# Two unused constant tables added and two gaps between on-chip tensors removed, in a two-layer-pair transformer kernel

## The reference

```python
for l in range(2):                                   # first kind ("one")
    mod = silu(c) @ ada_w[l] + ada_b[l]              # 9 x 1024 shifts, scales, gates
    h += 0.5 * g1 * swiglu(modulate(rms_norm(h)), ffn1_w_in[l], ffn1_w_out[l])
    z = modulate(rms_norm(h)) @ w_in[l]              # differential attention, convolution,
    h += g2 * concat(o_a, o_b, o_c, o_d) @ w_out[l]  # spatial gating, forgetting attention
    h += 0.5 * g3 * swiglu(modulate(rms_norm(h)), ffn2_w_in[l], ffn2_w_out[l])
for l in range(2):                                   # second kind ("two")
    z = rmsnorm(h) @ w_in_2[l]                       # 24 heads of q, k, v and 3 x 1024 gates
    h += (gates * branches) @ w_o_2[l]               # dilated, block and stick-breaking attention
    h += relu(rmsnorm(h) @ w_up_2[l]) ** 2 @ w_down_2[l]
```

## Time and profile before

| what | value |
|---|---|
| time, median of 3 runs | 2022.61 us (2020.84, 2022.61 and 2032.96) |
| the profiled execution's own time | 2022.61 us |
| span of its trace | 2020.8 us |
| mean granted TensorE clock | 0.982 of full |
| PE busy | 1944.2 us (96%), 15216 matmuls |
| POOL busy | 1320.6 us (65%) |
| ACT busy | 940.4 us (47%) |
| DVE busy | 835.4 us (41%) |
| bytes read by DMA | 394.62 MB, 196 GB/s over the span |

### The profile page before, as it was taken

The page is one execution under the profiler, slowest core; times in us unless marked ns, Lnnn a source line. Parts: engine busy times, 40 slices in busy tenths (PEclk is TensorE's granted clock), DMA queues, the critical chain, the costliest instruction groups (busy, mean ns, idle before and its releaser), DMA issues.

```text
span 2020.8 us, 36133 instructions
## 1 busy us (share of the span) xinstructions
PE 1944.2 (96%) x15216; PEld 1870.4 (93%) x15216; DVE 835.4 (41%) x1747; ACT 940.4 (47%) x1467; POOL 1320.6 (65%) x612
## 2 busy tenths in 40 slices
PE   7999997999999999889999999999999999999999
PEld 3999996899999999779999999989999999989999
DVE  3774577382147466745112622233311622233322
ACT  2544454344454445444444445525543445525543
POOL 0888760388878887316887964506897964505896
PEclk8999998999999999899999999999999999999999
DMA  9999650695589885217545643336664643335662
GB/s 321 359 345 308 198 185 22 207 365 181 185 302 365 279 264 187 84 63 267 192 161 173 209 157 110 125 118 189 200 204 152 209 148 112 124 121 188 199 201 99
DMA packets 357075, 398.01 MB, mean 197 GB/s; under 512 B 9017, under 2 KB 319025, under 8 KB 356913
## 3 DMA queue, kind: packets, MB, share of 16 engines
q1 hardware_dynamic: 356752, 395.50, 59.0%
q10 hardware_dynamic: 160, 0.20, 0.0%
HBM read 394.62 MB, written 1.05 MB: 196 GB/s over the span
## 4 chain that ended last, share of the span: by engine, by line
PE 85%; DVE 4%; SPq 3%; ACT 3%; POOL 2%; DMA 1%; issue 1%; ACTq 0%; DVEq 0%
PE bank L716 67%; PE bank L800 6%; PE bank L1124 3%; POOL w_lo L682 2%; PE bank L929 1%; PE bank L963 1%; SPq L577 1%; SPq L544 1%; DVE bank L1653 1%; PE bank L747 1%; ACT w_hi L1204 1%; DVE arena L1724 1%; PE bank L751 1%; PE bank L1025 1%; SPq L587 1%
## 5 line engine op out<-in xcount | busy, mean ns | idle before, releaser
L682 POOL TENSOR_TENSOR w_lo<-ring,w_hi 128x1024 fp32r<-128x1024 f32 (+2 forms) x608 | 1320.4, 2197 | 685.3 <-ACT w_hi L1204 684.7
L716 PE MATMUL bank<-hn,w_hi 128*128 128x256 f32 x2752 | 773.5, 281 | 5.9 <-POOL w_lo L682 5.0
L1204 ACT ACTIVATE w_hi<-ring 128x1024 fp32r<-128x1024 f32 (+2 forms) x608 | 578.5, 976 | 409.9 <-PE bank L716 368.2
L716 PE MATMUL bank<-hn_lo,w_hi 128*128 128x256 f32 x2752 | 764.8, 278 | 0.0
L716 PE MATMUL bank<-hn,w_lo 128*128 128x256 f32 x2752 | 764.7, 278 | 0.0
L716 PEld LDWEIGHTS bank<-hn,w_hi 128*128 128x128 f32 x2752 | 519.5, 189 | 10.1 <-POOL w_lo L682 6.0
L716 PEld LDWEIGHTS bank<-hn_lo,w_hi 128*128 128x128 f32 x2752 | 518.5, 188 | 1.2 <-issue 0.5
L716 PEld LDWEIGHTS bank<-hn,w_lo 128*128 128x128 f32 x2752 | 518.0, 188 | 0.0
L716 PE MATMUL bank<-gated,w_hi 128*128 128x256 f32 x1408 | 248.9, 281 | 0.0
L716 PEld LDWEIGHTS bank<-gated,w_hi 128*128 128x128 f32 x1408 | 217.0, 190 | 0.0
L716 PE MATMUL bank<-gated,w_lo 128*128 128x256 f32 x704 | 197.8, 281 | 0.0
(11 more groups left out here) (209 smaller groups left out, 2226.1 us busy)
## 6 DMA issues: line engine op xcount, KB each, us to landing
ring<-in_ffn_w_in SPq DMA_DIRECT2D x88, 1024.0 KB, 7.5
ring<-in_w_in SPq DMA_DIRECT2D x72, 1024.0 KB, 5.1
arena<-in_ada_w SPq DMA_DIRECT2D x35, 2048.0 KB, 10.5
ring<-in_w_up SPq DMA_DIRECT2D x32, 1024.0 KB, 5.4
ring<-in_w_down SPq DMA_DIRECT2D x32, 1024.0 KB, 5.1
ring<-in_ffn_w_out SPq DMA_DIRECT2D x32, 768.0 KB, 5.1
ring<-in_ffn_w_out SPq DMA_DIRECT2D x32, 640.0 KB, 4.1
ring<-in_w_in SPq DMA_DIRECT2D x16, 512.0 KB, 3.6
```

The source lines that it names most:

```text
L682: pool.tensor_tensor(w_lo[:, q, ks], ring[:, r, k0:k0 + n], w_hi[:, q, ks], ALU.subtract) \
L716: last = mm(out, a, b, start=start and i == 0, stop=stop and i == 2)
L1204: f(w_hi[:, q, half * 4:half * 4 + n], ring[:, r, k0:k0 + n], ACT.Copy).then_inc(weights_rounded, 1)
```

## The change

The host's table gains a block "before" of 384 columns ahead of "before_neg", and a block "in64" of 2 columns ahead of "in64_eighth". The two unused tensors `hn_start` and `arena_start` go. No instruction is added, removed or moved on any engine, and no wait.

```diff
@@ constant_tables
     before = np.concatenate([before[:P, :], before[P:, P:]], axis=1)
+    put("before", before)
     put("before_neg", np.where(before > 0, 0.0, -2.0 ** 100))
     put("in32", r[:, None] // 32 == np.arange(4)[None, :])
+    put("in64", r[:, None] // 64 == np.arange(2)[None, :])
     put("in64_eighth", (r[:, None] // 64 == np.arange(2)[None, :]) * 0.125)
@@ build
         h = sb("h", KT, S)
-        hn_start = sb("hn_start", 48)
         hn, hn_lo = sb("hn", KT, S, dtype=F32R), sb("hn_lo", KT, S, dtype=F32R)
@@ build
         ident_r, unseen = sb("ident_r", P, dtype=F32R), sb("unseen", P, dtype=F32R)
-        arena_start = sb("arena_start", 80)
         arena = sb("arena", ARENA)
```

## The result

| | before | after |
|---|---|---|
| median | 2027.07 us (4 runs, 2020.84 to 2032.96) | 2055.74 us (4 runs, 2053.22 to 2056.45) |
| the profiled execution | 2022.61 us, span 2020.8 | 2055.16 us, span 2053.4 |

The kernel became slower: the ratio is 1.014, with a 95% interval of 1.0121 to 1.016. The forecast was 2023.2 us, between 2016 and 2037, with no change that can be measured. Both were wrong, and rival A, equal offsets collide, is what happened.

The account below looks back on a forecast made before the run. PE's three-part products at line 716 were taken to bound the kernel, with DMA at the start. 2022.61 us plus 0 for addresses plus 0.6 for table bytes gave 2023.2 us, range 2016 to 2037 us.

Parts of the forecast that it names:

- rival A: Matmuls with `hn`: weight load and moved operand at equal offsets collide, up to 43 us, giving 2066 us; chance 0.14.
- What bounds the kernel: Whole span: PE busy 96%, 85% of the chain, line 716 alone 67%; slower matmuls there count in full.
- The offset of either operand alone is worth nothing: Line 716: offsets 192 and 704 go at 113.3 to 113.4 ns, offset 0 at 114 ns, so 0 us.
- Do equal offsets matter? I take 0 us.: `hn` against its weights: 0 us, since plain float32 takes 215 ns at equal and 216 ns at unequal offsets.
- The upper bound: Most that equal offsets could cost: 4.5 ns for each of 9600 matmuls with `hn` or `hn_lo`, 43 us.
- The bound for a gain: Slow stretches of line 716 all at the fast pace: 13.4 us in the long pieces, perhaps some 20 us.
- The rule of two read ports: TensorE reads the moved operand and the weight load through independent ports, so equal offsets would cost nothing.
- Two paces, set by the last interruption: Line 716 goes at 113.3 or 117.9 ns, set by what interrupted PE last, not by where operands lie.
- The bytes, 0.6 us.: Start, SP's table loads: 197,632 bytes more at 350 GB/s, 0.6 us in full on the path, 1.2 at most.
- DVE and ACT: Reads and writes of `hn`, `square`, `const` and tables at new addresses: 0 us, any cost hidden anyway.
- Rival B: Stretches of line 716 fall out at the other pace: one turned gives 2020 or 2027 to 2030 us; chance 0.20.
- C: Stretches with `hn` lose the slow pace: up to some 20 us faster, 2003 us; chance 0.05.

Follow-up runs that it names:

- tables-alone kernel: The changed kernel with the gap of 48 float32 ahead of `hn` kept and the new table 8 columns narrower; 2034.41 us, ratio 1.0061 against before.

## Why the prediction was wrong

*What bounds the kernel* held: outside the start, each nanosecond of a matmul in line 716 came out in the time in full, and nothing else did.

*The offset of either operand alone is worth nothing.* This held, and more strictly than I had shown it: the same `hn` address is fast against weights at 0 and slow against weights at 192.

*Do equal offsets matter? I take 0 us.* This is the step that failed: the term for equal offsets, put at nothing. The row it stood on, plain float32 at 215 and 216 ns, is true, and holds at all seven offsets that the runs have, but it doesn't carry over to the three-part form. That the load has some 100 ns more to hide there (215 against 113 ns from start to start) may be why; that is argued and was not tried. For the three-part form the price is 6.7 ns over the fast pace and 2.2 over the slow one. I had named the row as weaker than the case asked for, and then drew a chance of 0.14 from it, when the trace said that each pairing it had shown in this form stood at 192 or 64 within 256 bytes, all the good ones. A trace that holds none but the good offsets says nothing about the others. The sign that the prediction gave for A came out to the letter: long pieces with `hn` over 115 ns a matmul, with `up2` still at 113.

*The upper bound* of 4.5 ns for each of 9600 matmuls, 43 us, was the right count with two wrong sizes that partly cancel. The step is 6.7 ns from the fast pace, not 4.5; but those that came from the slow pace, such as the 912 at 583.49 us, lost only 2.2, and 2112 of `gated` gained 4.5 each, 9.5 us. I had not thought of that gain. A's price at half its bound, 2045 us, and its full price, 2066 us, stand on either side of the 2055.74 measured; that it lies so well between them is luck. The bound for a gain had missed the second `x624`, at 691.72 us, which makes it 16.2 us for the long pieces and not 13.4.

*The rule of two read ports* (the Trainium skill, TensorE: Matmul & The Clock Gate, "Step-by-step: what each phase is for") says that loading the next weights doesn't take bandwidth from the running matmul. The runs disagree for this form: the same two streams of reads take 113.3, 117.8, 118.7 or 120.0 ns a matmul by nothing but their offsets. The measurement decides. For plain float32 the runs agree with the rule, with the same 27.88 us for 128 at seven offsets. Whether there are two ports no run here shows; in the three-part form the two streams aren't free of each other.

*Two paces, set by the last interruption* held in part: an interruption turned the pace, but the same one left the piece of 912 slow in one run and fast in another. And it misled me in one place: I concluded from it that the pace is no matter of where operands lie. It is a matter of both. At offsets of 64 and 192 the interruption chooses among two, at 0 and 96 there is only the slow one of 120.

*The bytes, 0.6 us.* The loads read 893.5 KB as foretold:

```profile
const<-in_constants SPq DMA_DIRECT2D x2, 893.5 KB, 14.1
```

but they cost next to nothing. In the tables-alone kernel the last wait for DMA ended 0.2 to 0.4 us later and a faster piece of 96 made up for it. In the changed kernel PE is slower in that stretch and no longer waits for chunks at all:

```profile
126.00:163.00 37.00, 37.00 (x311) 37.00 (x310) 21.12 (x29) 16.83 (x20) 30.93 (x14) 1.00 1.05 345
```

PE is busy for the whole 37 us, where it had 35.63 before. So the start lost only 1.6 us although 912 matmuls went from mostly 113.3 to 120.0 ns: part of the slower pace took the place of waits.

*DVE and ACT* at 0 held (their busy times above). Not all moves are multiples of 64 bytes, as one sentence has it: the tables behind "in64" move by 1352, as another says. It made no difference.

*Rival B*, a stretch that falls out otherwise, is real too, as the spread of the kernel before; it would also account for the median of 2027.07 in this comparison, for the 2022.61 from which the sum was made, though those runs have no profile that shows it. *C* is out, as a gain for `hn`; its argument, that `gated`'s relation doesn't change and so its pace wouldn't, failed: `gated` has the fast pace in all four of its long pieces now, behind an `hn` at 120.0 ns.

## What to carry to other kernels

Where PE streams short matmuls of the rounded form back to back, and each needs its own weights, the start address of the moved tensor against the weights' buffer is a tuning knob worth up to 6% of the matmul pace (113.3 to 120.0 ns; 256 columns is the only length tried). With plain float32 it isn't one. A gap of a few dozen float32 that looks like waste, or a constant table that grows ahead of such a tensor, can turn it. Keep the relation fixed by allocating the two next to each other or by an assert, check it in the trace by the time from start to start over a long piece, and don't conclude from one good relation that the others are as good.

## What the runs showed of the hardware

- At the full granted clock, three-part matmuls of 256 columns with a load of 128 columns beside each go at 113.3 ns at best. By the relative offset of moved operand and loaded weights they go at up to 120.0 ns, with a period not over 256 bytes; 0 and 96 were the worst, 64 and 192 the only ones with 113.3.
- The collision is with the load that runs beside the matmul, that of the next matmul's weights, as far as the mean of the one kernel for it tells (120.0 against 115.6 or 118.5 ns). The mechanism below that, whether banks of SBUF or something else, stays open, and so does why 96 is as bad as 0 and 32 isn't.
- At offsets of 64 and 192 there are two stable paces, 113.3 and 117.8 ns. Small matmuls of 0.80 us in between turned the first into the second for the following 1152, in both layers of the one run. The same piece of 912 had either pace in two runs. What turns it back for sure wasn't found.
- Plain float32 matmuls of 256 columns (215 to 216 ns) don't show any of this: 128 take 27.88 us with the moved operand at 0, 32, 96, 160, 192, 224 and 256 against its weights.
